# Centring the value vectors of an RWKV-7 recurrence before the recurrence, in place of centring its outputs

## The reference, cut to what matters

```python
def step(state, inp):
    r_t, w_t, k_t, v_t, a_t, b_t = inp
    sa = jnp.einsum('bhij,bhj->bhi', state, a_t)
    state = (state * w_t[:, :, None, :] + sa[..., None] * b_t[:, :, None, :]
             + v_t[..., None] * k_t[:, :, None, :])
    y = jnp.einsum('bhij,bhj->bhi', state, r_t)
    return state, y
...
y = rwkv7_recurrence(rh, heads(decay), kh, vh, -kk, kk * ah)
mean = jnp.mean(y, axis=-1, keepdims=True)
var = jnp.mean(jnp.square(y - mean), axis=-1, keepdims=True)
y = ((y - mean) * lax.rsqrt(var + LNX_EPS)).reshape(B, S, R) * lnx_g + lnx_b
bonus = (jnp.sum(rh * kh * r_k, axis=-1, keepdims=True) * vh).reshape(B, S, R)
return (y + bonus) * g * jax.nn.silu(z)
```

## Time and profile before

| | |
|---|---|
| Median of 3 runs | 3076.42 us (3075.11 to 3078.22) |
| Span of the profiled execution, first to last instruction | 3078.5 us |
| PE busy | 2993.1 us, 97% |
| DVE busy | 1357.8 us, 44% |
| ACT busy | 1185.6 us, 39% |
| POOL busy | 1636.4 us, 53% |
| Mean granted TensorE clock | 0.987 of full speed |

### The profile page before, as it was taken

How to read it: one execution, slowest core, us unless ns; L and a number is a source line. 1 busy time by engine, 2 the same in 40 slices (tenths; PEclk the granted TensorE clock), 3 DMA queues, 4 the chain that set the end, 5 groups by cost and what they waited for, 6 DMA issues and landing times.

```text
span 3078.5 us, 53450 instructions
## 1 busy us (share of the span) xinstructions
PE 2993.1 (97%) x21200; PEld 2379.8 (77%) x21200; DVE 1357.8 (44%) x2156; ACT 1185.6 (39%) x1631; POOL 1636.4 (53%) x1355
## 2 busy tenths in 40 slices
PE   7899999999899999999999999999999999998997
PEld 5778788888788888888888877777777777775686
DVE  8788861120343132222322046455456455465612
ACT  5355652243543232323333254343343343344521
POOL 4455544454667777777773464444444444344252
PEclk9999999999999999999999999999999999998998
DMA  4567674232222222222222242222222222225522
GB/s 171 169 195 205 196 194 154 96 149 96 83 90 89 99 89 85 89 98 89 89 86 95 96 148 97 84 99 75 87 103 75 90 91 87 90 75 149 170 98 96
DMA packets 128903, 347.32 MB, mean 113 GB/s; under 512 B 61920, under 2 KB 64992, under 8 KB 98288
## 3 DMA queue, kind: packets, MB, share of 16 engines
q1 hardware_dynamic: 128752, 345.08, 33.7%
HBM read 305.41 MB, written 34.90 MB: 111 GB/s over the span
## 4 chain that ended last, share of the span: by engine, by line
PE 49%; issue 25%; POOL 19%; DVE 4%; ACT 2%; DMA 1%; SPq 0%; POOLq 0%; DVEq 0%; ACTq 0%
POOL wlo L172 16%; PE bank L195 14%; PE bank L197 14%; PE bank L196 14%; POOL g L1990 2%; PE bank L1407 1%; PE bank L1389 1%; PE bank L2084 1%; POOL wk L643 1%; PE bank L1398 1%; DMA wraw<-in_wall_dram 1%; PE bank L2158 0%; PE bank L2124 0%; POOL wk L637 0%; ACT whi L167 0%
## 5 line engine op out<-in xcount | busy, mean ns | idle before, releaser
L172 POOL TENSOR_TENSOR wlo<-wraw,whi 128x512 fp32r<-128x512 f32 (+1 forms) x896 | 1182.4, 1350 | 1188.5 <-ACT whi L167 1188.3
L195 PE MATMUL bank<-rhi,whi 128*128 128x512 f32 x3632 | 1458.6, 402 | 45.6 <-POOL wlo L172 30.6
L196 PE MATMUL bank<-rlo,whi 128*128 128x512 f32 x3632 | 1422.0, 392 | 0.0
L197 PE MATMUL bank<-rhi,wlo 128*128 128x512 f32 x3632 | 1421.9, 391 | 0.0
L195 PEld LDWEIGHTS bank<-rhi,whi 128*128 128x128 f32 x3632 | 685.1, 189 | 219.3 <-issue 39.3
L197 PEld LDWEIGHTS bank<-rhi,wlo 128*128 128x128 f32 x3632 | 685.2, 189 | 145.6
L196 PEld LDWEIGHTS bank<-rlo,whi 128*128 128x128 f32 x3632 | 686.3, 189 | 136.9 <-issue 4.3
L167 ACT ACTIVATE whi<-wraw 128x2048 fp32r<-128x2048 f32 (+2 forms) x227 | 428.2, 1887 | 457.3 <-PE bank L197 273.9
L1181 POOL TENSOR_TENSOR wraw<-wraw,vec 128x512 f32<-128x512 f32 x248 | 252.0, 1047 | 0.0
L960 DVE TENSOR_TENSOR ssum<-ssum,wk 128x512 f32<-128x512 f32 x28 | 20.6, 737 | 278.1 <-ACT wk L950 278.1
L1990 POOL TENSOR_TENSOR g<-g,wk 128x256 f32<-128x256 f32 x80 | 58.8, 755 | 108.9 <-PE bank L1765 57.4
(11 more groups left out here) (381 smaller groups left out, 3049.1 us busy)
## 6 DMA issues: line engine op xcount, KB each, us to landing
wraw<-in_wall_dram SPq DMA_DIRECT2D x223, 1024.0 KB, 4.9
g<-in_bmat_dram SPq DMA_DIRECT2D x16, 512.0 KB, 4.0
g<-scr_e SPq DMA_DIRECT2D x128, 64.0 KB, 3.1
scr_a<-ssum SPq DMA_DIRECT2D x24, 256.0 KB, 2.3
g<-in_xp_dram SPq DMA_DIRECT2D x4, 1024.0 KB, 12.3
g<-in_cmat_dram SPq DMA_DIRECT2D x16, 256.0 KB, 7.2
scr_u<-wk SPq DMA_DIRECT2D x16, 256.0 KB, 2.7
scr_y<-wk SPq DMA_DIRECT2D x16, 256.0 KB, 3.2
```

Source lines behind the costliest of these rows:

```text
L172: ins = pool.tensor_tensor(wlo[:, slot, c], wraw[:, slot, c], whi[:, slot, c].bitcast(F32), ALU.subtract)
L195: pe.matmul(out[:, :], whk, rhi[:, k, :], start=(k == first), stop=False)
L196: pe.matmul(out[:, :], whk, rlo[:, k, :], start=False, stop=False)
L197: ins = pe.matmul(out[:, :], wlk, rhi[:, k, :], start=False, stop=(k == last))
```

## The change

The four transposes of v still go to bank 7. Where ACT copied that bank into `vt`, DVE now sums it per head (a `tensor_reduce` of 128 x 8 x 64) and writes `vt` as the bank minus a 64th of the sum. This stands in DVE's order between L1589 and L1592. The bonus still takes the values as they were (`w["v"]`). At the end of a pass ACT squares the outputs from PSUM into `s_hi` and `kk` and copies them into `lc`, six half instructions in a row; the first head sum, the subtraction of the mean and the two later squares are gone. The fills around the sum left over are joined.

```diff
+        def value_center(d, link, p):
+
+            by_head = banks[7].rearrange("p (g i) -> p g i", g=2 * NB)
+            d.wait_ge(rw_tv, p + 1)
+            link(d.tensor_reduce(xt["st"][:, 0:2 * NB], by_head, AX.X, ALU.add))
+            d.scalar_tensor_tensor(w["vt"].rearrange("p (g i) -> p g i", g=2 * NB), bc(xt["st"][:, 0:2 * NB], 2, [P, 2 * NB, CH]),
+                                   -1 / CH, by_head, ALU.mult, ALU.add).then_inc(rw_vc, 1)
...
                             per_head(w["lc"])[:, 1:NC_, CH // 2 - 1], ALU.add).then_inc(rw_lc, 1)
+            value_center(d, link, p)
             d.wait_ge(rw_nr, p + 1)
...
-            ys, cn = w["ys"], w["lc"]
-            d.wait_ge(rw_yc, p + 1)
-            sum_low(d, ys).then_inc(rw_sl, 1)
-            d.wait_ge(rw_mu, p + 1)
-            d.scalar_tensor_tensor(cn, banks[6][:, :], -1 / CH, ys, ALU.mult, ALU.add).then_inc(rw_cn, 1)
+            d.wait_ge(rw_cs, p + 1)
+            sum_low(d, w["kk"]).then_inc(rw_sl, 1)
             if not nxt:
-                d.wait_ge(rw_cs, p + 1)
-                sum_low(d, w["kk"]).then_inc(rw_sl, 1)
                 xb_add(d, 2)
                 return
             rw_inputs(d, link, p + 1, 0)
-            d.wait_ge(rw_cs, p + 1)
-            sum_low(d, w["kk"]).then_inc(rw_sl, 1)
             rw_inputs(d, link, p + 1, 1)
...
-            fill(6 if nxt else 3)
-            pe.wait_ge(rw_sl, 4 * p + 3)
-            head_sum(pe, banks[6]).then_inc(rw_mu, 1)
-            fill(7 if nxt else 4)
-            pe.wait_ge(rw_sl, 4 * p + 4)
+            fill(8 if nxt else 5)
+            pe.wait_ge(rw_sl, 3 * p + 3)
             head_sum(pe, banks[7]).then_inc(rw_vr, 1)
-            if nxt:
-                fill(128)
+            fill(128 if nxt else 2)
...
             hi(0)
-            act.wait_ge(rw_tv, p + 1)
-            act.activation(w["vt"], banks[7][:, :], ACT.Copy).then_inc(rw_vc, 1)
             act.wait_ge(rw_n2, p + 1)
...
             act.wait_ge(rw_ym, p + 1)
-            for e in range(2):
-                of = banks[2 + e][:, 0:HB].rearrange("p (b t) -> p b t", b=NB)
-                act.activation(ys4[:, :, e], of, ACT.Copy)
-                ins = act.activation(s_hi.rearrange("p (b e t) -> p b e t", b=NB, e=2)[:, :, e], of, ACT.Copy)
-            ins.then_inc(rw_yc, 1)
+            for out, f in ((s_hi, ACT.Square), (w["kk"], ACT.Square), (w["lc"], ACT.Copy)):
+                for e in range(2):
+                    of = banks[2 + e][:, 0:HB].rearrange("p (b t) -> p b t", b=NB)
+                    ins = act.activation(out.rearrange("p (b e t) -> p b e t", b=NB, e=2)[:, :, e], of, f)
+            ins.then_inc(rw_cs, 1)
...
             hi(5)
-            act.wait_ge(rw_cn, p + 1)
-            act.activation(w["kk"], w["lc"], ACT.Square)
-            act.activation(s_hi, w["lc"], ACT.Square).then_inc(rw_cs, 1)
             act.wait_ge(rw_vr, p + 1)
...
             if h == 1:
-                pe.wait_ge(rw_cn, 8)
                 pe.wait_ge(rw_sd, 8)
```

More of the change, by code:

```diff
@@ L1419, in program @@
                       ("ar", 2 * T), ("bh", T), ("kh", T), ("bt", T), ("kt", T), ("vt", T), ("sh", T)])
-        w["ys"], w["at"], w["rv"], w["wt"], w["uh"] = w["lw"], w["a"], w["kk"], w["t1"], w["t2"]
+        w["at"], w["rv"], w["wt"], w["uh"] = w["a"], w["kk"], w["t1"], w["t2"]
         HB = T // 2
@@ L1436, in program @@
         gi4 = w["gi"].rearrange("p (b e t) -> p b e t", b=NB, e=2)
-        ys4 = w["ys"].rearrange("p (b e t) -> p b e t", b=NB, e=2)
         hs_ = [slice(0, CH), slice(CH, P)]
@@ L1477, in program @@
         rw_ym = sem("rw_ym")
-        rw_yc = sem("rw_yc")
-        rw_mu = sem("rw_mu")
-        rw_cn = sem("rw_cn")
         rw_cs = sem("rw_cs")
@@ L1724, in rw_pe @@
             ins.then_inc(rw_tv, 1)
-            pe.wait_ge(rw_sl, 4 * p + 1)
+            pe.wait_ge(rw_sl, 3 * p + 1)
             head_sum(pe, banks[5]).then_inc(rw_n2, 1)
@@ L1751, in rw_pe @@
             transposes(5, lambda b: w["bh"][:, b * P:(b + 1) * P])
-            pe.wait_ge(rw_sl, 4 * p + 2)
+            pe.wait_ge(rw_sl, 3 * p + 2)
             head_sum(pe, banks[6]).then_inc(rw_bm, 1)
@@ L2706 @@
 EARLY_SQ = 6
-RW_LINKS = 18
+RW_LINKS = 19
 (V_G1, V_SGN, V_HPI, V_EPS6, V_EPS5, V_RND, V_RNM, V_ONE, V_BF, V_BG, V_GPOST0, V_GKV, V_GPRE, V_GPOST1, V_G2, V_GF,
```

## The result

The changed kernel takes **3086.98 us** (median of 6 runs, 3084.26 to 3090.62), the kernel before beside it 3077.32 us (6 runs, 3072.5 to 3080.37): a ratio of **1.0029**, 95% interval 1.0019 to 1.0039, some 9 us slower. The profiled span grew from 3078.5 to 3088.8 us, by 10.3.

A forecast was written before the change was run, and what follows sets the result against it. PE bounds the kernel: its work and the places where it stands. 8 x 1.6 + 7 x (1.01 - 0.31 - 0.46) - 1.2 = +13.3 us on the median of 3076.42 gives 3089.7 us, range 3082 to 3094.

The forecast's parts named there:

- DVE's front part: DVE before `rw_op`: reduce 0.68, subtraction 0.69; L1592 starts about 2021.98, ends about 2023.5, reciprocal at 2023.55 instead of 2021.11.
- the first rival: `lo(0)` on POOL: L1592 still slips in ahead of the fourth piece; L1607 1.3 late, +8.9 us, 3085.3; chance 0.25.
- Whatever is put into this chain comes out at its end: DVE, L1589 to L1607: it never waits for another engine there, so added time comes out at L1607; no separate size.
- `lo(1)`: DVE beside POOL: four instructions stretched until about 2033.2, L1607 1.85 us late, PE stands 1.6 in each of 8 passes, +12.8.
- slack: At `rw_op`, DVE's L1607 ends ahead of PE's L1742 start; 0.25 us of lateness there costs PE nothing.
- Tile 6: End of a pass: `hi(5)` 0.53 late behind six halves, `lo(5)` 0.48 more from DVE; +1.01 us in each of 7 passes.
- Tile 7: End of a pass: PE's wait for `lo(6)` goes, since the remaining sum and root come sooner; -0.31 us, 7 times.
- the head sum: PE's work at the end of a pass: two matmuls go, -0.46 us a pass.
- The end of the eighth pass: Before the attention: the last sum no longer waits for a late low part; L2084 starts at 2801.25, not 2802.45, -1.2 us.
- The attention: Behind the stage: the wait for `rw_cn` goes but `rw_sd` beside it holds as before; zero.
- More port waits: DVE's reduce and subtraction also take turns with POOL; L1607's lateness saturates near 2.0; +17.2 us, 3093.6; chance 0.10.
- The pair is hidden: At `rw_op`: L1607's lateness stays under 0.25 us, no loss there; +0.5 us in all, 3076.9; chance 0.07.

The follow-up runs named there:

- the copy: Changed kernel with one tensor_copy of bank 7 to vt replacing DVE's reduce and subtraction, centring left out: median 3079.99 us, ratio 1.001 to the kernel before.
- the doubled reduce: Changed kernel with DVE's tensor_reduce done twice, 0.68 us more on its chain in each pass: ratio 1.0029 to the kernel before.

## Why the prediction was right, and where a size was off

It was made at +13.3 us; the medians moved by +9.7 and the spans by +10.3. The time lies in the range, and the mechanism was the forecast's own; which of two close branches came true was in part luck.

- **DVE's front part** came out to hundredths. On the clock of the trace before (minus 1.38), L1597 starts at 2021.96 (forecast 2021.98), ends at 2023.48 (2023.5), the reciprocal starts at 2023.52 (2023.55), and `lo(1)` meets L1599 first. Reduce and broadcast took the prices of the nearest forms, 0.68 and 0.69. Which piece L1597 would meet hung on hundredths, as the first rival said. The third and fourth piece of `lo(0)`, on POOL's timeline:

```profile
2022.04 1.29 POOL L172 TENSOR_TENSOR wlo<-wraw,whi 128x512 fp32r<-128x512 f32 x1
...
2023.30 1.29 POOL L172 TENSOR_TENSOR wlo<-wraw,whi 128x512 fp32r<-128x512 f32 x1
```

  L1597 starts at 2023.34, 0.01 us behind the end of the third (2022.04 + 1.29 = 2023.33). All eight passes fall on this side, but no row of the kernel before could decide 0.01 us: that the forecast came true and not the first rival is luck to that extent.
- **"Whatever is put into this chain comes out at its end"** does not hold. The pair puts in 1.3 us and L1612 is 1.49 late; with a second reduce 2.0 go in and it is 1.49 late again; the copy puts in 0.6 and 0.90 comes out. The sum did not go by this sentence but by the pieces.
- **`lo(1)`: the term that was mis-sized.** The step said that four met instructions run "until about 2033.2" and the last operand is 1.85 us late. It is 1.49 late (20.29 us behind the chain's first instruction for 18.80), since the four end at 2032.93: they take 1.20, 1.27, 1.66 and 1.54 us, not 1.5 to 1.8 each. The first meets a piece that had already run for 0.63 us (2027.66 to 2028.29), and `lo(1)` as a whole takes 6.11 us, not 6.55. With a slack of 0.28, taken as 0.25 (PE starts 0.10 us behind L1612's end, where the estimates were 0.05 and up to 0.2), that makes 1.21 a pass and not 1.6; the eighth stands 1.68. Together 7 x 1.21 + 1.68 = **10.2 us for 12.8**.
- **Tile 6**, +1.03 for +1.01, by the two parts given: 0.53 for `hi(5)` and 0.47 for `lo(5)`.
- **Tile 7 and the head sum.** The wait went and the sum went. Beside the 0.31 and 0.46 the slower stream behind the stall went too, 0.13, which had not been counted. So a pass grew by 1.26 and not by 1.21 + 1.01 - 0.31 - 0.46 = 1.45; some 0.1 of the difference was not taken apart.
- **The end of the eighth pass** was 1.9 us shorter, not 1.2: the sum had L2084 (now L2072) wait for the input of the earlier trace rows, but by the end of the longer stage that input was there, and PE runs into the attention without a wait. POOL's timeline of the changed kernel:

```profile
2808.98 2.00 POOL L2057 TENSOR_TENSOR wk<-wk 128x1024 f32<-128x1024 f32 x1 [1.53 <-DMA wk<-scr_a]
```

PE's:

```profile
2810.82 0.39 PE L197 MATMUL bank<-rhi,wlo 128*128 128x512 f32 x1
2811.14 2.42 PE L2072 MATMUL bank<-wk 64*128 64x512 f32 x8
```

- **The attention** behind it was priced at zero, and took 1.5 us more, which brings the sum nearer to the forecast by luck. In PE's timeline two waits for the softmax's division on DVE, of 1.08 and 0.71 us (L2112, released by L2103), stand there that the trace before does not have. The same stretch takes 93.1 to 94.5 us in the profiles of the six experiments that share the changed kernel's attention, so it swings by over a microsecond with the same code. Why was not tried; it stays open.
- **The rivals.** "Slips in ahead of the fourth piece" is what the copy alone does: 0.62 us of stall a pass, where the forecast gave that case 1.05, too much for the same reason as above. "More port waits" predicted that the loss saturates; the doubled reduce shows that it does, already at the changed kernel's 1.21; its condition did not come true, for the pair took no turn (0.68 and 0.69 us beside `lo(0)`). "The pair is hidden" held for no run in which the pair stood there and POOL did all its work.

## What to carry to other kernels

In this kernel an instruction put into a chain that runs beside POOL is not priced by its duration but by the POOL piece behind which the next instruction with its operands in SBUF comes to stand: here 0.6 us cost 0.6, 1.3 us cost 1.2, and 2.0 us also 1.2 a pass. Before a step is put in front of a wait's last operand, look for a time in which that engine waits anyway; moving the same two instructions ahead of a wait for ACT, and a weight's rounding ahead of a wait for PE, turned a change of +9.7 us into one of about -8.7 (3067.07 for 3075.72 on the same chip; some 2 us of it the early rounding gives the kernel before as well). Where the profile puts a wait down to "issue", find its releaser by time on the other engines' timelines.

## What the runs showed that was not expected

- A `tensor_reduce` of 0.68 us added to each pass in a chain that ends at PE's stall cost 0.3 us in seven passes, all of it in one pass and away from the stall.
- An instruction on 128x7 elements took 1.25 us beside POOL and 0.16 where the pieces were left out: its turn cost 1.1 us, as much as that of L1597 on 128x512 (1.52 for 0.41).
- Removing the stall at tile 6 gained 0.1 us a pass more than the stall's length, in the matmuls behind it (1.33 us for 1.21); at `rw_op` it did not (8.6 us over seven passes for 8.5).
